# Turning the hidden blocks of the SwiGLU layers on TensorE in place of VectorE blocks and GpSimd transfers

## The chip, the cores and the metric

The kernel runs as one program on one core of a Trainium2 chip. The metric is the device time of one launch in microseconds (us), lower is better. Engines are named as the profile names them: PE is TensorE (PEld its weight loads), DVE is VectorE, ACT is ScalarE, POOL is GpSimd, SP is SyncE, which here only issues transfers. PSUM is the accumulator memory that PE writes; it has 8 banks of 512 float32 per partition (`ps[:, bank, :]` in the code).

## The reference

A two-layer decoder trunk on 256 tokens of width 2048: an RWKV-7 time-mixing layer, then a block-sparse attention layer, and after each mixer a layer norm, a SwiGLU feed-forward network and another layer norm. The change is in the feed-forward part alone:

```python
def _swiglu(x, w_gate, w_up, w_down):
    return (jax.nn.silu(x @ w_gate) * (x @ w_up)) @ w_down

for layer in range(DEPTH):          # DEPTH = 2
    mixed = ...                     # RWKV-7 in layer 0, attention in layer 1
    h = _layernorm(ALPHA * h + mixed, ln1_w[layer], ln1_b[layer])
    h = _layernorm(ALPHA * h + _swiglu(h, ffn_w_gate[layer], ffn_w_up[layer], ffn_w_down[layer]),
                   ln2_w[layer], ln2_b[layer])
```

`x` is 256 x 2048, `w_gate` and `w_up` are 2048 x 5632, `w_down` is 5632 x 2048, all float32.

## The kernel before

**Matmuls.** All projections have one form. A weight matrix is cut into chunks of 256 rows by 512 columns (512 KB, two row tiles of 128). A job is one output block of 512 columns for all 256 tokens: 8 chunks where the inner size is 2048 (`CJ`), 22 where it is 5632 (`CF`). Precision is kept by splitting both operands into a high and a low part of type float32r: each product is three matmuls, high by high, high by low and low by high (`chunk`, L629 to L644, lines L641, L642, L643). The activations are the 128x128 stationary operand, the weights the 512 moving columns, so a chunk is 2 row tiles x 2 token tiles x 3 = 12 matmuls of 512 columns. Odd and even jobs write PSUM banks 0 and 1, or 2 and 3.

**The ring of weights.** SP loads the chunks into a ring of four slots, `raw` (L355, and L397 for `w_down`). ACT copies each to its high part `whi` (`split_hi`, L1310), once it has landed (`raw_landed`) and PE has used the chunk four before it (`chunk_used`). DVE subtracts to get the low part `wlo` (`split_lo`, L1761; in the down projection the same operation in `residual`, L2095) and signals `split_done`, which PE waits for ahead of each chunk and which frees the slot of `raw` for SP.

**The feed-forward part.** For each layer the stage `up` works on the 5632 hidden columns in 11 blocks of 512 (`FB`). A block is two jobs: the gate job into banks 0 and 1, the up job into banks 2 and 3. After the gate job ACT computes Silu of the banks into `gtmp` (token on the partitions, L1636; block 0 has the same operation outside the loop). After the up job DVE multiplies `gtmp` by the other two banks (`multiply`, L2198). The down projection needs the result with the hidden index on the partitions, as stationary operand: `hThi` and `hTlo`. So each block of 256 tokens x 512 hidden columns is turned:

- DVE turns 32x32 squares within each partition group, two instructions for the two token tiles, into `hB` (L2201), and signals `h_blocked`.
- POOL issues 16 transfers from SBUF to SBUF per block, which carry the squares to the right partitions, into `hR` (`turn_hidden`, L605); they signal `h_landed`.
- ACT copies `hR` to the high part `hThi` (`hidden_hi`, L1620), and DVE subtracts for `hTlo` (`hidden_lo`, L2206), which signals `hlo_done`.

Block 0 of a layer is made by `normed_job`, ahead of a loop of 10 (`Fori(0, FB - 1)`) for blocks 1 to 10. ACT and DVE turn block i while PE works on block i + 1: `hidden_hi` stands right behind Silu of the next block in ACT's queue. Block 10 is turned during the down projection: its `hidden_hi` comes after `BEHIND` = 8 further chunks in ACT's queue, and PE needs its result at chunk 20 of 22 of the first down job. The squares leave the hidden index in a permuted order, four hidden rows to a partition; so SP loads `w_down` in the matching order (`blocks`, L392 to L398).

**What sets the order.** Each engine runs its queue in the order written; semaphores tie them together. PSUM banks 4 to 7 are used by the layer norms' turns (`turned`, L1141, PE transposes of 128x128 float32), and by attention, whose PE transposes (L1202) stand between the chunks of the q and output projections. They are idle in the stages `up` and `down`. The whole program has 8 stages in the order proj, wo, up0, down0, kvq, ao, up1, down1.

Of the kernel before, what the change touches and what calls it, by code (L numbers as in the profile page):

```python
# [23 lines left out]
F32 = mybir.dt.float32  # L24
F32R = mybir.dt.float32r
ALU = mybir.AluOpType
# [3 lines left out]
P = 128  # L30
D = 2048
T = 256
# [7 lines left out]
KC = 2  # L40
RING = 4
PLAIN = 2
BEHIND = 8
# [118 lines left out]
def trunk(nc, x, rows, rwkv_rows, lora, w, consts, ln_rows, y):  # L162
    with ExitStack() as ctx:
# [117 lines left out]
        hB = carve(common, 16 * KB, 16, TT, 32)  # L281
        hR = carve(common, 20 * KB, 4, 4, TT, 32)
# [58 lines left out]
        h_blocked, h_landed, hhi_done, hlo_done = (sem(n) for n in ("h_blocked", "h_landed", "hhi_done", "hlo_done"))  # L341
# [8 lines left out]
        def _(sp):  # L350
# [36 lines left out]
            def blocks(c0, mats, kt, n, n0=0):  # L387

                per = len(mats) * kt // KC
                if per % RING:  # L390
                    with sp.Fori(0, n // 2) as i:
                        for b in range(2):  # L392
                            for j in range(kt // KC):
                                c = b * (kt // KC) + j
                                rows = mats[0][j // 2 * 4 * P:(j // 2 + 1) * 4 * P, bass.ds(i * (2 * NB) + (n0 + b) * NB, NB)]
                                sp.wait_ge(split_done, i * (2 * per) + (c0 + c) - (RING - 1))
                                sp.dma_start(raw[:, c % RING], rows.rearrange("(p k) n -> p k n", k=4)[:, j % 2 * KC:(j % 2 + 1) * KC]  # L397
                                             ).then_inc(raw_landed[c % RING], 16)  # L398
                else:
                    with sp.Fori(0, n) as i:  # L400
                        stream(i * per + c0, mats, kt, bass.ds(i * NB + n0 * NB, NB))
# [68 lines left out]
        def _(pool):  # L470
# [129 lines left out]
            def turn_hidden(i):  # L600

                pool.wait_ge(h_blocked, i + 1)
                for a in range(4):
                    for q in range(4):
                        nc.gpsimd.dma_start(hR[32 * q:32 * (q + 1), a], hB[32 * a:32 * (a + 1), 4 * q:4 * (q + 1)]).then_inc(h_landed, 16)  # L605

            for t in range(TT):
                root(0, t)
            for i in range(FB):
                turn_hidden(i)  # L610
# [7 lines left out]
            for i in range(FB, 2 * FB):  # L618
                turn_hidden(i)
# [10 lines left out]
        def _(pe):  # L630
# [539 lines left out]
            def ffn(layer):  # L1170
                c0, j0 = PH[f"up{layer}"]
                u0 = layer * FB

                normed_job(2 * layer, f"up{layer}")
                with pe.Fori(0, FB - 1) as i:
                    job(i * (2 * CJ) + (c0 + 2 * CJ), i + (j0 // 2 + 1), 0, KT, ahi, alo)
                    job(i * (2 * CJ) + (c0 + 3 * CJ), i + (j0 // 2 + 1), 1, KT, ahi, alo)
                c, j = PH[f"down{layer}"]
                pe.wait_ge(hlo_done, u0 + FB - 1)
                pe.wait_ge(bank_free[0], j // 2 + 1)  # L1180
                for ch in range(CF):
                    if ch == CF - KC:
                        pe.wait_ge(hlo_done, u0 + FB)
                    chunk(c, ch, 0, FT, hThi, hTlo)
                job(c + CF, j // 2, 1, FT, hThi, hTlo)
                last_two(c + 2 * CF, j + 2, FT, hThi, hTlo)
# [109 lines left out]
        def _(act):  # L1296
# [317 lines left out]
            def ffn(layer):  # L1614
# [3 lines left out]
                def hidden_hi(i, f0):  # L1618
                    act.wait_ge(h_landed, i * 256 + 256)
                    A(hThi[:, f0, :].rearrange("p f (t a j) -> p f t a j", t=TT, a=4), hR.rearrange("p a f t j -> p f t a j"),  # L1620
                      ACT.Copy).then_inc(hhi_done, 1)
# [7 lines left out]
                with act.Fori(0, FB - 1) as i:  # L1629
# [4 lines left out]
                    act.wait_ge(h_blocked, i + (u0 + 1))  # L1634
# [5 lines left out]
                split_hi(c, c // RING, BEHIND)  # L1640
                hidden_hi(u0 + FB - 1, slice((FB - 1) * 4, FB * 4))
                split_hi(c + BEHIND, c // RING, NJ * CF - RING - BEHIND - layer * 2 * RING)
# [85 lines left out]
        def _(dve):  # L1728
# [349 lines left out]
            def residual(c0, kt, n):  # L2078
# [6 lines left out]
                at = c0 + RING + {0: 9, 1: BEHIND, 2: 2 * CJ - RING, 3: BEHIND}[n]  # L2085
# [104 lines left out]
            def ffn(layer):  # L2190
# [3 lines left out]
                def multiply(c_end, up_seen):  # L2194

                    dve.wait_ge(bank_free[0], up_seen)
                    dve.wait_ge(chunk_used, c_end)
                    V.tensor_tensor(gtmp, gtmp, ps[:, 2:4, :], ALU.mult).then_inc(bank_free[1], 1)  # L2198
                    dve.wait_ge(bank_free[1], up_seen)
                    for t in range(TT):  # L2200
                        last = V.transpose(hB[:, :, t], gtmp[:, t].rearrange("p (q i f) -> p q f i", q=4, f=4))  # L2201
                    last.then_inc(h_blocked, 1)

                def hidden_lo(i, f0):
                    dve.wait_ge(hhi_done, i + 1)
                    V.tensor_tensor(hTlo[:, f0, :].rearrange("p f (t a j) -> p f t a j", t=TT, a=4), hR.rearrange("p a f t j -> p f t a j"),  # L2206
                                    hThi[:, f0, :].bitcast(F32).rearrange("p f (t a j) -> p f t a j", t=TT, a=4),
                                    ALU.subtract).then_inc(hlo_done, 1)
# [9 lines left out]
                split_lo(PH[f"down{layer}"][0] + RING, BEHIND)  # L2218
# [122 lines left out]
```

## Time and profile before

| what | value |
|---|---|
| time, median of 3 runs | 2440.54 us (2440.26 to 2443.91) |
| the profiled execution's own time | 2440.26 us |
| its span, first to last instruction | 2438.5 us |
| PE busy | 2418.4 us, 99% |
| DVE busy | 1443.3 us, 59% |
| ACT busy | 1068.9 us, 44% |
| POOL busy | 309.7 us, 13% |
| mean traffic | 186 GB/s, 452.45 MB |

The span is 1.8 us shorter than the execution's own time, which has what lies before the first and after the last instruction. The matmul durations in the profile are latencies of a pipeline: they overlap, so how fast PE works is read from the starts of its instructions, which follow each other at a smaller distance than one lasts. The stage up0 runs in the trace from 593 us (the transposes of its layer norm) to 1077, down0 from 1077 to 1317, up1 from 1705 to 2188, and down1 from there to the end. Attention's transposes between chunks lie between 1520 and 1640 us.

### The profile page before, as it was taken

How to read it: one execution, taken by the hardware profiler on the slowest of the kernel's cores; microseconds unless marked ns; L12 is line 12 of the kernel's file. 1: busy time of each engine (PE TensorE's matmuls, PEld its weight loads, DVE VectorE, ACT ScalarE, POOL GpSimd, SP SyncE). 2: the span in 40 equal slices, each digit the busy share in tenths (PEclk: the TensorE clock that was granted, in tenths of full speed). 3: DMA queues.
4: the chain of work that ended last, by engine and by line, in shares of the span. 5: the costliest groups of instructions: out<-in, count | busy, mean ns of one | idle time of the engine just before them, and what ended most of it. 6: DMA issues, size and time to landing. Idle time of an engine off the chain costs nothing.

```text
span 2438.5 us, 39415 instructions
## 1 busy us (share of the span) xinstructions
PE 2418.4 (99%) x15364; PEld 1983.1 (81%) x15364; DVE 1443.3 (59%) x1725; ACT 1068.9 (44%) x1345; POOL 309.7 (13%) x536
## 2 busy tenths in 40 slices
PE   9999999999999999999999999999999999999998
PEld 6888778877888888888887888888788888888886
DVE  7788566666755555555446544665855555555445
ACT  4454455444444444444334444553544444444332
POOL 2000235420112121120000000000111212111000
PEclk9999999999999999999999999999999999999999
DMA  7556411266666666666666665455666766667664
GB/s 240 189 192 212 131 42 46 59 211 200 200 204 209 200 204 207 205 208 195 194 192 208 199 195 192 141 177 183 188 202 204 208 204 208 202 203 233 194 195 147
DMA packets 237774, 452.45 MB, mean 186 GB/s; under 512 B 19328, under 2 KB 31040, under 8 KB 236560
## 3 DMA queue, kind: packets, MB, share of 16 engines
q1 hardware_dynamic: 222304, 417.38, 55.3%
q0 software_dynamic: 14944, 33.11, 4.2%
q8 instruction: 91, 1.49, 0.2%
q14 instruction: 35, 0.29, 0.0%
q10 hardware_dynamic: 400, 0.18, 0.0%
HBM read 436.96 MB, written 2.10 MB: 180 GB/s over the span
## 4 chain that ended last, share of the span: by engine, by line
PE 97%; DMA 2%; DVE 1%; issue 0%; ACT 0%; POOL 0%; SPq 0%; DVEq 0%; ACTq 0%
PE ps L643 26%; PE ps L641 26%; PE ps L642 26%; PE ps L965 3%; PE ps L858 1%; PE ps L846 1%; PE ps L1151 1%; PE ps L668 1%; PE ps L670 1%; PE ps L669 1%; PE ps L909 1%; PE ps L811 1%; PE ps L955 1%; DMA raw<-w_k 1%; PE ps L1251 1%; PE ps L992 1%
## 5 line engine op out<-in xcount | busy, mean ns | idle before, releaser
L1310 ACT CAST whi<-raw 128x1024 fp32r<-128x1024 f32 x738 | 775.9, 1052 | 1131.4 <-PE ps L643 1070.5
L1761 DVE TENSOR_TENSOR wlo<-raw,whi 128x1024 fp32r<-128x1024 f32 x569 | 691.9, 1222 | 583.1 <-ACT whi L1310 580.9
L641 PE MATMUL ps<-whi,ahi 128*128 128x512 f32 x2184 | 855.1, 392 | 0.0
L643 PE MATMUL ps<-whi,alo 128*128 128x512 f32 x2184 | 850.7, 390 | 0.0
L642 PE MATMUL ps<-wlo,ahi 128*128 128x512 f32 x2184 | 850.4, 389 | 0.0
L642 PEld LDWEIGHTS ps<-wlo,ahi 128*128 128x128 f32 x2184 | 410.2, 188 | 85.7 <-issue 1.2
L641 PEld LDWEIGHTS ps<-whi,ahi 128*128 128x128 f32 x2184 | 410.2, 188 | 85.5 <-issue 1.2
L643 PEld LDWEIGHTS ps<-whi,alo 128*128 128x128 f32 x2184 | 410.2, 188 | 85.1
L2095 DVE TENSOR_TENSOR wlo<-raw,whi 128x1024 fp32r<-128x1024 f32 x179 | 219.0, 1224 | 227.4 <-ACT whi L1310 226.1
L605 POOL DMA_DIRECT2D common<-common x352 | 172.0, 497 | 818.0 <-DVE common L2201 739.1
L641 PE MATMUL ps<-whi,hThi 128*128 128x512 f32 x656 | 255.4, 389 | 0.0
L642 PE MATMUL ps<-wlo,hThi 128*128 128x512 f32 x656 | 255.4, 389 | 0.0
L643 PE MATMUL ps<-whi,hTlo 128*128 128x512 f32 x656 | 255.4, 389 | 0.0
L643 PEld LDWEIGHTS ps<-whi,hTlo 128*128 128x128 f32 x656 | 123.2, 188 | 25.6
L641 PEld LDWEIGHTS ps<-whi,hThi 128*128 128x128 f32 x656 | 123.2, 188 | 25.5
L642 PEld LDWEIGHTS ps<-wlo,hThi 128*128 128x128 f32 x656 | 123.2, 188 | 25.3
L595 POOL TENSOR_TENSOR rstd<-var,small 128x1 f32<-128x1 f32 x8 | 5.3, 665 | 582.7 <-DVE var L2133 582.7
L965 PE MATMUL ps<-raw,big 128*128 128x256 f32 x256 | 68.8, 400 | 0.1
L965 PEld LDWEIGHTS ps<-raw,big 128*128 128x128 f32 x256 | 44.5, 189 | 7.5 <-ACT big L1456 0.2
L1593 ACT ACTIVATE a2t<-ps,lnT 128x128 f32<-128x128 f32 x96 | 33.8, 549 | 30.7 <-PE ps L1141 30.7
L1926 DVE TENSOR_TENSOR rec<-ps,big 128x512 f32<-128x512 f32 x40 | 27.5, 688 | 32.6 <-PE ps L846 32.6
L2201 DVE STREAM_TRANSPOSE common<-common 128x512 f32<-128x512 f32 x44 | 45.2, 1066 | 0.8
(317 smaller groups left out, 1937.6 us busy)
## 6 DMA issues: line engine op xcount, KB each, us to landing
raw<-w_up SPq DMA_DIRECT2D x176, 512.0 KB, 4.4
raw<-w_down SPq DMA_DIRECT2D x176, 512.0 KB, 4.0
raw<-w_gate SPq DMA_DIRECT2D x172, 512.0 KB, 3.7
raw<-w_k SPq DMA_DIRECT2D x32, 512.0 KB, 4.3
raw<-w_r SPq DMA_DIRECT2D x32, 512.0 KB, 4.3
raw<-w_v SPq DMA_DIRECT2D x32, 512.0 KB, 3.6
raw<-w_o SPq DMA_DIRECT2D x32, 512.0 KB, 4.8
raw<-kv_v SPq DMA_DIRECT2D x32, 512.0 KB, 3.6
```

The costliest lines, as they stand in the source:

```text
L605: nc.gpsimd.dma_start(hR[32 * q:32 * (q + 1), a], hB[32 * a:32 * (a + 1), 4 * q:4 * (q + 1)]).then_inc(h_landed, 16)
L641: mm(o, hi[:, k, tok], whi[:, s, k2, :], start=(k == 0), stop=False)
L642: mm(o, hi[:, k, tok], wlo[:, s, k2, :], start=False, stop=False)
L643: last = mm(o, lo[:, k, tok], whi[:, s, k2, :], start=False, stop=(k == kt - 1))
L668: mm(ps[:, 2 + t, :], hi[:, k, tok], wh[:, k2, :], start=False, stop=False)
L965: last = mm(ps[:, 3, t * T:(t + 1) * T], xxT[:, k, t * P:(t + 1) * P], rawf[:, s, k % FK], start=(i == 0), stop=(k == KT - 1), skip_group_ ...
L1310: nc.scalar.copy(whi[:, s], src).then_inc(hi_done, 1)
L1593: ins = A(hF[:, k, t * P:(t + 1) * P], ps[:, 4 + b, k2 * P:(k2 + 1) * P], ACT.Identity, scale=lnT[:, (n * 2) * KT + k:(n * 2) * KT + k + 1 ...
L1761: V.tensor_tensor(wlo[:, s], src, whi[:, s].bitcast(F32), ALU.subtract).then_inc(split_done, 1)
L1926: V.tensor_tensor(Z.rearrange("p l (j c) -> p l j c", c=CHUNK), ps[:, 0:2, 0:4 * CHUNK].rearrange("p l (j c) -> p l j c", c=CHUNK), mask_l ...
L2095: V.tensor_tensor(wl, raw[:, s], wh.bitcast(F32), ALU.subtract).then_inc(split_done, 1)
L2201: last = V.transpose(hB[:, :, t], gtmp[:, t].rearrange("p (q i f) -> p q f i", q=4, f=4))
```

## The change

The turn of a hidden block moves to PE. A new function `h_transposes(i)` issues 8 transposes of 128x128 (4 hidden tiles x 2 token tiles) from `gtmp` into banks 4 and 5, after a wait for the multiply (`bank_free[1]`), and signals `h_tr`. In the loop it stands between the gate job and the up job; for the last block, between chunks 1 and 2 of the first down job. ACT's `hidden_hi` and DVE's `hidden_lo` now read the banks in place of `hR`. The Silu of the next block waits for `h_tr` where it waited for `h_blocked`, and PE waits at the end of each turn of the loop for `hlo_done`, which says that the banks have been read. DVE's two square turns per block and POOL's 16 transfers per block go, with their buffers. The order of the hidden index is now the plain one, so `w_down` is loaded like every other matrix, and for block 10 `hidden_hi` and `hidden_lo` come after 1 further chunk in place of 8.

```diff
--- before.py
+++ after.py
@@ -40,7 +40,6 @@
-BEHIND = 8
@@ -278,8 +277,6 @@
-        hB = carve(common, 16 * KB, 16, TT, 32)
-        hR = carve(common, 20 * KB, 4, 4, TT, 32)
@@ -338,7 +335,7 @@
-        h_blocked, h_landed, hhi_done, hlo_done = (sem(n) for n in ("h_blocked", "h_landed", "hhi_done", "hlo_done"))
+        h_tr, hhi_done, hlo_done = (sem(n) for n in ("h_tr", "hhi_done", "hlo_done"))
@@ -392,10 +389,8 @@
                         for b in range(2):
                             for j in range(kt // KC):
                                 c = b * (kt // KC) + j
-                                rows = mats[0][j // 2 * 4 * P:(j // 2 + 1) * 4 * P, bass.ds(i * (2 * NB) + (n0 + b) * NB, NB)]
-                                sp.wait_ge(split_done, i * (2 * per) + (c0 + c) - (RING - 1))
-                                sp.dma_start(raw[:, c % RING], rows.rearrange("(p k) n -> p k n", k=4)[:, j % 2 * KC:(j % 2 + 1) * KC]
-                                             ).then_inc(raw_landed[c % RING], 16)
+                                chunk(i * (2 * per) + (c0 + c), c % RING,
+                                      mats[0][j * KC * P:(j + 1) * KC * P, bass.ds(i * (2 * NB) + (n0 + b) * NB, NB)])
                 else:
                     with sp.Fori(0, n) as i:
                         stream(i * per + c0, mats, kt, bass.ds(i * NB + n0 * NB, NB))
@@ -597,17 +592,8 @@
             load_wb(0, z_tr, KT // KC)
             nc.gpsimd.memset(small[:, 0:1], -0.5).then_inc(half_set, 1)
             pool.wait_ge(half_set, 1)
-            def turn_hidden(i):
-
-                pool.wait_ge(h_blocked, i + 1)
-                for a in range(4):
-                    for q in range(4):
-                        nc.gpsimd.dma_start(hR[32 * q:32 * (q + 1), a], hB[32 * a:32 * (a + 1), 4 * q:4 * (q + 1)]).then_inc(h_landed, 16)
-
             for t in range(TT):
                 root(0, t)
-            for i in range(FB):
-                turn_hidden(i)
             root(1, 0)
             load_wb(1, chunk_used, PH["kvq"][0])
             root(1, 1)
@@ -615,8 +601,6 @@
             load_wb(2, qk_tr, STEPS)
             for t in range(TT):
                 root(2, t)
-            for i in range(FB, 2 * FB):
-                turn_hidden(i)
             pool.wait_ge(chunk_used, PH["down1"][0])
             nc.gpsimd.dma_start(wb_last, lnw(3)).then_inc(wb_in, 16)
             for t in range(TT):
@@ -1171,10 +1155,20 @@
                 c0, j0 = PH[f"up{layer}"]
                 u0 = layer * FB
 
+                def h_transposes(i):
+
+                    pe.wait_ge(bank_free[1], i + (j0 // 2 + 2 - u0))
+                    for f in range(4):
+                        for t in range(TT):
+                            last = tr(ps[:, 4 + f // 2, (f % 2) * T + t * P:(f % 2) * T + (t + 1) * P], gtmp[:, t, f * P:(f + 1) * P], ident[:])
+                    last.then_inc(h_tr, 1)
+
                 normed_job(2 * layer, f"up{layer}")
                 with pe.Fori(0, FB - 1) as i:
                     job(i * (2 * CJ) + (c0 + 2 * CJ), i + (j0 // 2 + 1), 0, KT, ahi, alo)
+                    h_transposes(i + u0)
                     job(i * (2 * CJ) + (c0 + 3 * CJ), i + (j0 // 2 + 1), 1, KT, ahi, alo)
+                    pe.wait_ge(hlo_done, i + (u0 + 1))
                 c, j = PH[f"down{layer}"]
                 pe.wait_ge(hlo_done, u0 + FB - 1)
                 pe.wait_ge(bank_free[0], j // 2 + 1)
@@ -1182,6 +1176,8 @@
                     if ch == CF - KC:
                         pe.wait_ge(hlo_done, u0 + FB)
                     chunk(c, ch, 0, FT, hThi, hTlo)
+                    if ch == 1:
+                        h_transposes(u0 + FB - 1)
                 job(c + CF, j // 2, 1, FT, hThi, hTlo)
                 last_two(c + 2 * CF, j + 2, FT, hThi, hTlo)
 
@@ -1616,9 +1612,8 @@
                 u0 = layer * FB
 
                 def hidden_hi(i, f0):
-                    act.wait_ge(h_landed, i * 256 + 256)
-                    A(hThi[:, f0, :].rearrange("p f (t a j) -> p f t a j", t=TT, a=4), hR.rearrange("p a f t j -> p f t a j"),
-                      ACT.Copy).then_inc(hhi_done, 1)
+                    act.wait_ge(h_tr, i + 1)
+                    A(hThi[:, f0, :], ps[:, 4:6, :].rearrange("p a (k t) -> p (a k) t", k=2), ACT.Copy).then_inc(hhi_done, 1)
 
                 split_hi(c0 + RING, c0 // RING + 1, CJ)
                 act.wait_ge(chunk_used, c0 + CJ)
@@ -1631,15 +1626,15 @@
                     u = i * (2 * CJ // RING) + (c0 + 2 * CJ) // RING
                     split_hi(c + RING, u + 1, CJ)
 
-                    act.wait_ge(h_blocked, i + (u0 + 1))
+                    act.wait_ge(h_tr, i + (u0 + 1))
                     act.wait_ge(chunk_used, c + CJ)
                     A(gtmp, ps[:, 0:2, :], ACT.Silu).then_inc(bank_free[0], 1)
                     hidden_hi(i + u0, bass.ds(i * 4, 4))
                     split_hi(c + (RING + CJ), u + (1 + CJ // RING), CJ)
                 c = PH[f"down{layer}"][0] + RING
-                split_hi(c, c // RING, BEHIND)
+                split_hi(c, c // RING, 1)
                 hidden_hi(u0 + FB - 1, slice((FB - 1) * 4, FB * 4))
-                split_hi(c + BEHIND, c // RING, NJ * CF - RING - BEHIND - layer * 2 * RING)
+                split_hi(c + 1, c // RING, NJ * CF - RING - 1 - layer * 2 * RING)
 
             norm_affine(0, PH["up0"][0])
             ffn(0)
@@ -2082,7 +2077,7 @@
-                at = c0 + RING + {0: 9, 1: BEHIND, 2: 2 * CJ - RING, 3: BEHIND}[n]
+                at = c0 + RING + {0: 9, 1: 1, 2: 2 * CJ - RING, 3: 1}[n]
@@ -2196,16 +2191,11 @@
                     dve.wait_ge(bank_free[0], up_seen)
                     dve.wait_ge(chunk_used, c_end)
                     V.tensor_tensor(gtmp, gtmp, ps[:, 2:4, :], ALU.mult).then_inc(bank_free[1], 1)
-                    dve.wait_ge(bank_free[1], up_seen)
-                    for t in range(TT):
-                        last = V.transpose(hB[:, :, t], gtmp[:, t].rearrange("p (q i f) -> p q f i", q=4, f=4))
-                    last.then_inc(h_blocked, 1)
 
                 def hidden_lo(i, f0):
                     dve.wait_ge(hhi_done, i + 1)
-                    V.tensor_tensor(hTlo[:, f0, :].rearrange("p f (t a j) -> p f t a j", t=TT, a=4), hR.rearrange("p a f t j -> p f t a j"),
-                                    hThi[:, f0, :].bitcast(F32).rearrange("p f (t a j) -> p f t a j", t=TT, a=4),
-                                    ALU.subtract).then_inc(hlo_done, 1)
+                    V.tensor_tensor(hTlo[:, f0, :], ps[:, 4:6, :].rearrange("p a (k t) -> p (a k) t", k=2),
+                                    hThi[:, f0, :].bitcast(F32), ALU.subtract).then_inc(hlo_done, 1)
 
                 natural_and_split(2 * layer, c0)
                 with dve.Fori(0, FB - 1) as i:
@@ -2215,7 +2205,7 @@
                     hidden_lo(i + u0, bass.ds(i * 4, 4))
                     split_lo(c + (RING + CJ), CJ)
                 multiply(c0 + FB * 2 * CJ, j0 // 2 + FB + 1)
-                split_lo(PH[f"down{layer}"][0] + RING, BEHIND)
+                split_lo(PH[f"down{layer}"][0] + RING, 1)
                 hidden_lo(u0 + FB - 1, slice((FB - 1) * 4, FB * 4))
 
             residual(PH["wo"][0], KT, 0)
```

On PE, at the end of the gate job in the loop of the stage up0. The kernel before (L641 to L643 are the matmuls of `chunk`, L636 the wait of the next job):

```order
L641 MATMUL ps<-whi,ahi 128x512
L642 MATMUL ps<-wlo,ahi 128x512
L643 MATMUL ps<-whi,alo 128x512
L636 REGISTER_ALU [waits bank_free1]
L641 MATMUL ps<-whi,ahi 128x512 [waits split_done]
```

The changed kernel, at the same place (L625 to L627 are the matmuls of `chunk`, `common` is the memory in which `gtmp` lies):

```order
L625 MATMUL ps<-whi,ahi 128x512
L626 MATMUL ps<-wlo,ahi 128x512
L627 MATMUL ps<-whi,alo 128x512
L1163 MATMUL ps<-ident,common 128x128 [waits bank_free1]
L1163 MATMUL ps<-ident,common 128x128 x7
L620 REGISTER_ALU [waits bank_free1]
L625 MATMUL ps<-whi,ahi 128x512 [waits split_done]
```

Eight instructions, the first with a wait, stand between the two jobs; nothing else on PE has moved.

On ACT, after the loop, at the start of the down projection of layer 0. The kernel before (L1310 is the copy of a chunk's high part, L1620 is `hidden_hi` of block 10):

```order
L1310 CAST whi<-raw 128x1024 [waits chunk_used,raw_landed2]
L1310 CAST whi<-raw 128x1024 [waits chunk_used,raw_landed3]
L1620 ACTIVATE hThi<-common 128x1024 [waits h_landed]
L1310 CAST whi<-raw 128x1024 [waits chunk_used,raw_landed0]
L1310 CAST whi<-raw 128x1024 [waits chunk_used,raw_landed1]
```

The changed kernel, from the end of the loop (L1624) on (L1306 is the copy, L1616 is `hidden_hi`):

```order
L1624 REGISTER_ALU
L1624 COMPARE_AND_BRANCH
L1306 CAST whi<-raw 128x1024 [waits chunk_used,raw_landed0]
L1616 ACTIVATE hThi<-ps 128x1024 [waits h_tr]
L1306 CAST whi<-raw 128x1024 [waits chunk_used,raw_landed1]
```

`hidden_hi` of block 10 is now the second operation after the loop, behind one copy; before, eight copies stood ahead of it.

## Rows read from the trace of the kernel before

**Rows 1.** The page: busy time, granted clock by slice of the span.

```profile
PE 2418.4 (99%) x15364; PEld 1983.1 (81%) x15364; DVE 1443.3 (59%) x1725; ACT 1068.9 (44%) x1345; POOL 309.7 (13%) x536
...
PEclk9999999999999999999999999999999999999999
```

**Rows 2.** Stretches: busy us and instructions (x) by engine, clock, DMA share, GB/s.

```profile
560.00:640.00 80.00, 80.00 (x356) 63.93 (x355) 58.44 (x67) 37.80 (x58) 1.12 (x2) 1.00 0.60 186
640.00:1080.00 440.00, 440.00 (x1943) 364.54 (x1942) 239.91 (x203) 187.84 (x182) 78.25 (x160) 1.00 0.69 205
1345.00:1510.00 165.00, 165.00 (x730) 136.70 (x729) 81.16 (x65) 72.14 (x71) 0.00 (x0) 1.00 0.61 195
1510.00:1640.00 130.00, 129.99 (x657) 109.55 (x656) 80.85 (x106) 65.16 (x122) 0.53 (x1) 1.00 0.49 163
```

**Rows 3.** Waits from 640 to 1080 us: in total, times, longest.

```profile
ACT whi L1310 <- PE ps L643: 252.2, 152, 1.7
DVE wlo L1761 <- ACT whi L1310: 192.9, 132, 1.5
```

**Rows 4.** Timeline of PE, first transposes of attention: start, us, what.

```profile
1518.04 0.39 PE L643 MATMUL ps<-whi,alo 128*128 128x512 f32 x1
...
1520.08 0.39 PE L643 MATMUL ps<-whi,alo 128*128 128x512 f32 x1
1520.31 1.03 PE L1202 MATMUL ps<-ident,big 128*128 128x128 f32 x8
1521.10 0.48 PE L641 MATMUL ps<-whi,ahi 128*128 128x512 f32 x1
1521.41 0.40 PE L642 MATMUL ps<-wlo,ahi 128*128 128x512 f32 x1
...
1523.69 0.39 PE L643 MATMUL ps<-whi,alo 128*128 128x512 f32 x1
```

**Rows 5.** Timeline of PE, the next group of eight transposes.

```profile
1533.21 0.40 PE L643 MATMUL ps<-whi,alo 128*128 128x512 f32 x1
1533.44 1.04 PE L1202 MATMUL ps<-ident,big 128*128 128x128 f32 x8
...
1536.86 0.39 PE L643 MATMUL ps<-whi,alo 128*128 128x512 f32 x1
```

**Rows 6.** Line L1202, PE: duration ns min/median/max.

```profile
L1202 PE MATMUL ps<-ident,big x64: 270/273/276, 1520.3 to 1625.6; 128*128 128x128 f32 x64
```

**Rows 7.** Timeline of ACT, then of DVE: end of a gate job in up0.

```profile
661.20 1.05 ACT L1310 CAST whi<-raw 128x1024 fp32r<-128x1024 f32 x1 [1.67 <-PE ps L643]
663.92 1.05 ACT L1310 CAST whi<-raw 128x1024 fp32r<-128x1024 f32 x1 [1.67 <-PE ps L643]
664.87 1.02 ACT L1636 ACTIVATE common<-ps 128x1024 f32<-128x1024 f32 x1
665.79 1.05 ACT L1620 ACTIVATE hThi<-common 128x1024 f32 x1
666.74 1.04 ACT L1310 CAST whi<-raw 128x1024 fp32r<-128x1024 f32 x1
...
662.28 1.23 DVE L1761 TENSOR_TENSOR wlo<-raw,whi 128x1024 fp32r<-128x1024 f32 x1 [1.50 <-ACT whi L1310]
667.01 1.23 DVE L2206 TENSOR_TENSOR hTlo<-common,hThi 128x1024 f32 x1 [0.78 <-ACT hThi L1620]
```

**Rows 8.** Timeline of PE, DVE and ACT, start of down0.

```profile
1077.16 0.39 PE L641 MATMUL ps<-whi,hThi 128*128 128x512 f32 x1
...
1079.59 1.21 DVE L2198 TENSOR_TENSOR common<-common,ps 128x1024 f32<-128x1024 f32 x1
...
1082.85 1.05 ACT L1310 CAST whi<-raw 128x1024 fp32r<-128x1024 f32 x1 [1.67 <-PE ps L643]
```

**Rows 9.** The page: what the change takes out.

```profile
L605 POOL DMA_DIRECT2D common<-common x352 | 172.0, 497 | 818.0 <-DVE common L2201 739.1
L2201 DVE STREAM_TRANSPOSE common<-common 128x512 f32<-128x512 f32 x44 | 45.2, 1066 | 0.8
```

**Rows 10.** DMA issues: KB each, median us from issue to landing.

```profile
raw<-w_up SPq DMA_DIRECT2D x176, 512.0 KB, 4.4
raw<-w_down SPq DMA_DIRECT2D x176, 512.0 KB, 4.0
```

**Rows 11.** Timeline of PE, first layer norm's transposes, and what follows them.

```profile
603.46 0.79 PE L641 MATMUL ps<-whi,ahi 128*128 128x512 f32 x1
604.09 0.40 PE L642 MATMUL ps<-wlo,ahi 128*128 128x512 f32 x1
```

## Prediction, made before the changed kernel ran

> **What bounds the kernel now.** I read the page first, then a table of stretches, the waits inside one stretch, and the timeline of PE. The page shows PE busy for 99% of the span and its granted clock at the upper level, 2.4 GHz, in every slice [rows 1]. Durations of matmuls overlap, so the busy share alone could hide a slow stream. The starts do not: nine steps from 1518.04 to 1520.08 us make 2.04 us, 0.227 us for a matmul of 512 columns [rows 4]. The stretches say the same of the stage that is changed: 440 us hold 1943 matmuls, 0.226 us each, and the stretch from 1345 to 1510, in which POOL does nothing and no square is turned, holds 730 in 165 us, 0.226 us each [rows 2]. So beside DVE's turns and POOL's transfers PE runs as fast as without them. A chunk of 12 matmuls is 2.72 us.
>
> Who waits for whom between 640 and 1080 us: ACT waits 252.2 us for PE, in 152 pieces of up to 1.7 us, and DVE 192.9 us for ACT; no wait of PE is in the list [rows 3]. The ring is full and PE empties it. How far ahead it is: a copy starts at 661.20 us, DVE's subtraction behind it ends at 663.51 [rows 7], 2.3 us after the copy's start. The copy starts when PE has used one chunk, and PE needs the new one three chunks later, 8.2 us. The margin is about 5.8 us.
>
> **The change, part by part.**
>
> What goes: 44 square turns on DVE, 45.2 us, and 352 small transfers on POOL, 172.0 us of issuing [rows 9]. Neither engine sets the end, DVE is busy for 59% and POOL for 13% of the span [rows 1], and PE waits for neither in this stage. Worth on the path: nothing. If PE did wait for them unseen, it would show as a step above that of the stretch without them, and the step is the same [rows 2]. So the bounds of this term are 0 and 0.
>
> What comes: per block 8 transposes of 128x128 float32 on PE, which is the path itself. Nothing hides them. There are 10 blocks in the loop and one behind it, in two layers: 22 groups, 176 transposes. Attention has the same groups in the same surroundings: eight transposes of float32 against the identity into banks 4 and 5, between two float32r chunks. The price of a group can be read in three ways:
> - From the first transpose at 1520.31 to the second matmul after them at 1521.41 is 1.10 us, of which 0.227 is the step of a matmul: 0.87 us [rows 4].
> - From the last matmul before to the twelfth after them, 1520.08 to 1523.69, is 3.61 us; twelve steps are 2.72: 0.89 us [rows 4]. It has in it the few slightly longer steps that follow.
> - The same at the second group, 1533.21 to 1536.86: 3.65 less 2.72, 0.93 us [rows 5].
>
> I take 0.89, because the first group stands between plain jobs as the new ones will, while DVE and ACT do softmax work around the second. 22 x 0.89 = 19.6 us. The ends are 22 x 0.87 = 19.1 and 22 x 0.93 = 20.5 us.
>
> The waits that the change adds on PE:
> - `bank_free[1]` ahead of the transposes in the loop: the multiply is done right after the block's own up job, a whole gate job (21.8 us) before. Behind it on PE stands everything, but it is met.
> - The same ahead of the last group, in the down projection: PE starts down0 at 1077.16 and would reach the group after two chunks, at 1082.60; the multiply runs from 1079.59 to 1080.80 [rows 8]. Margin 1.8 us.
> - `hlo_done` at the loop's end: `hidden_lo` ends at 668.24 [rows 7]; the loop's end is a whole up job (21.8 us) behind the end of the gate job at 663.7, near 685.5. Margin 17 us.
>
> The waits on ACT: Silu now needs `h_tr`, 0.87 us after the end of the gate job. A copy starts at that end, at 663.92, so `h_tr` comes near 664.79; Silu starts behind that copy at 664.87 anyway [rows 7]. Behind it `hidden_hi` and the next copy keep their places, and that copy's chunk on PE is itself 0.87 us later. Cost 0.
>
> The reads of PSUM in place of SBUF: `hidden_hi` reads 1024 elements per partition from SBUF in 1.05 us, and Silu as many from PSUM in 1.02; `hidden_lo` takes 1.23 from SBUF, the multiply with one operand in PSUM 1.21 [rows 7, 8]. No difference, and off the path.
>
> `hidden_hi` of block 10, earlier in the queue: `h_tr` comes near 1082.60 + 0.87 = 1083.5, so the copy of chunk 5, which stood at 1082.85 [rows 8], starts near 1084.6 behind `hidden_hi`. DVE has `hidden_lo` between, and finishes the chunk near 1087.2. PE wants it at 1077.16 + 5 x 2.72 + 0.87 = 1091.6. Margin 4.4 us. The refill of that slot starts 2 us later than now, takes 4.0 us to land [rows 10], and its next copy has to wait for PE until about 1094.3. Cost 0. If these covers were gone, each microsecond of lateness would cost one, twice in the program.
>
> `w_down` in plain row order: the same 176 transfers of 512 KB, on the same queue; they land in 4.0 us now and those of `w_up`, which have the plain order, in 4.4 [rows 10]. The 0.4 us are inside the margin of the ring. Cost 0.
>
> Sum against the profiled execution: 2440.26 + 19.6 = 2459.9 us. The median of the three runs is 0.3 us above that execution, so 2460 us for the median.
>
> **The rivals.**
>
> 1. *A transpose costs its whole duration.* The row of the line gives 273 ns for one [rows 6]. If each stood alone on the engine, 176 x 0.273 = 48.0 us: 2488.3 us. Against it: the eight of a group stand in 0.79 us from the first start to the next matmul's [rows 4], 0.10 us each, so they overlap. It would take a reason for which those in the loop don't. I give it 3 in 100.
> The Trainium skill, in "TensorE: Matmul & The Clock Gate", Part 4: PE-mode transpose, gives about 275 ns for a transpose in a kernel's context, and says that transposes do not count as activity for the clock as matmuls do. By that rule the time would be that of this rival, with a fall of the clock possibly on top. The trace agrees with the duration and not with the cost, since the starts are 0.10 us apart; and the clock reads 1.00 both in the stretch of attention and in the one with 16 transposes in a row twice [rows 2].
>
> 2. *The change of kind is dearer in the loop.* After the layer norm's float32 work the first float32r matmul takes a step of 0.63 us (603.46 to 604.09) [rows 11], 0.40 more than usual, the dearest change of kind near this stage. In the loop the transposes also stand behind a wait against a register, which attention's don't have, and a second such wait closes the loop. If each group paid 0.40 more, 22 x 0.40 = 8.8: 2468.7 us. Against it: that step follows matmuls of 512 float32 columns, and eight transposes are followed by one of 0.31 [rows 4]; and each chunk begins with a wait in the same way now, with no mark on the step. 4 in 100.
>
> 3. *Not slower: PE's step is set by the supply of chunks.* If the ring delivered a chunk every 2.72 us, the transposes would fill time in which PE now waits, and the chunks would come when they come. It decides once a chunk becomes ready less than 0.87 us before its use. The time would then be 2440.3 us, or a little less, as POOL's transfers no longer share the DMA engines. For it: the DMA share is 0.69 in the stage, against 0.61 without the squares [rows 2]. Against it: the margin of 5.8 us, ACT waiting for PE and not for landings [rows 3], and the equal step in both stretches [rows 2]. 2 in 100.
>
> **How the numbers follow.** My forecast has 91 in 100: 2460 us, with 2459.4 to 2460.8 by the ends of the price, and a few tenths to a microsecond or two for things that I count as nothing. Rival 2 has 4, rival 1 has 3, rival 3 has 2. The range is 2457.5 to 2466: it takes in half of what rival 2 costs and leaves the rest out. A change of 0.2% is 4.9 us, about what a measurement of this kernel can tell from none. The forecast and rivals 1 and 2 lie above it, together 98; rival 3 is split between no change and faster, 1 each.
>
> **What would show each step.** In the profile of the changed kernel 176 transposes more on PE in 22 groups of 8, in the two stages up and at the start of each down projection. The start-to-start distance over a group and the twelve matmuls behind it should be 3.61 us. PE should have no idle time ahead of a group, the granted clock should stay at 1.00, the step elsewhere at 0.227 us, and each turn of the loop should be 0.89 us longer than 43.5. POOL should be idle in the stages, and DVE's busy time about 45 us lower. I am wrong if the groups cost much over 0.93 us, if the matmul step in other places changes, or if the span grows by another amount than the groups add up to.

## The result and the profile after

The changed kernel takes 2460.46 us (median of 6 runs, 2459.0 to 2461.51); the kernel before took 2440.4 us in its 6 (2437.9 to 2443.91). The ratio is 1.0081, with a 95% interval of 1.007 to 1.009. It is 20.1 us slower, and 2460 us were forecast.

The page of the changed kernel, busy time and what its transfers and DVE's turns left [rows 1, 9, 10]:

```profile
PE 2438.2 (99%) x15540; PEld 2000.3 (81%) x15540; DVE 1404.0 (57%) x1681; ACT 1071.2 (44%) x1345; POOL 137.6 (6%) x184
...
PEclk9999999999999999999999999999999999999999
...
raw<-w_up SPq DMA_DIRECT2D x176, 512.0 KB, 3.6
raw<-w_down SPq DMA_DIRECT2D x176, 512.0 KB, 4.1
```

PE has 176 instructions more and 19.8 us more busy time. DVE is 39.3 us lower, not 45 as forecast: the lengths of its instructions add up to 46.5 us less, but they overlap in part, less so here than before (46.1 us in all against 53.3). POOL is 172.1 us lower. The clock is the same.

The stretch of stage up0 and the one without transposes, of the changed kernel [rows 2], then the waits in the stage [rows 3]:

```profile
640.00:1080.00 440.00, 440.00 (x1983) 365.08 (x1982) 217.64 (x179) 185.30 (x179) 0.00 (x0) 1.00 0.65 189
...
1349.00:1514.00 165.00, 165.00 (x729) 136.64 (x728) 84.83 (x68) 72.86 (x71) 0.00 (x0) 1.00 0.61 195
```

```profile
ACT whi L1306 <- PE ps L627: 255.5, 159, 1.7
DVE wlo L1756 <- ACT whi L1306: 215.1, 159, 1.5
```

No wait of PE is in this list either. DVE now waits 22 us longer for ACT, about its 20.5 us of square turns in this stretch: it does nothing with the time that it got.

The timeline of PE at the first group of the loop, and at the second [rows 4, 5]:

```profile
664.90 0.39 PE L627 MATMUL ps<-whi,alo 128*128 128x512 f32 x1
665.13 1.03 PE L1163 MATMUL ps<-ident,common 128*128 128x128 f32 x8
665.92 0.48 PE L625 MATMUL ps<-whi,ahi 128*128 128x512 f32 x1
666.24 0.40 PE L626 MATMUL ps<-wlo,ahi 128*128 128x512 f32 x1
...
709.32 0.40 PE L627 MATMUL ps<-whi,alo 128*128 128x512 f32 x1
709.55 1.04 PE L1163 MATMUL ps<-ident,common 128*128 128x128 f32 x8
...
712.96 0.39 PE L627 MATMUL ps<-whi,alo 128*128 128x512 f32 x1
```

Nothing is idle ahead of the eight. From 709.32 to 712.96 are 3.64 us, which with the unrounded starts is 3.65: 0.93 us over twelve steps of 0.2267. The first group costs 0.89. From the first group to the second are 44.42 us (665.13 to 709.55) and from there to the third 44.44, against 43.52 for a turn of this loop in the kernel before: 0.9 more, as forecast. Over all 22 groups, measured in this way, the sum is 20.0 us: 12 groups of 0.89 and 10 of 0.93.

The profiled execution took 2461.66 us, 21.4 more than that of before. When the starts of PE's common instructions are laid side by side, the offset is 1.4 us from 600 us on, behind the first layer norm and ahead of anything that is changed; it grows by 0.89 or 0.93 at each of the 22 groups and elsewhere moves by less than 0.1 us. So 1.4 us is how two executions differ in their first stages, and 20.0 us is the change.

### The profile page after: what moved, and what is told of

Same layout as the page of the kernel before. It is cut to its first block, busy times and chain, and to the rows that moved or that the text cites. A ratio compares the mean times of both kernels' runs of the same rounds, so it can differ in the third digit from the quotient of the medians.

```text
span 2459.9 us, 39371 instructions
## 1 busy us (share of the span) xinstructions
PE 2438.2 (99%) x15540; PEld 2000.3 (81%) x15540; DVE 1404.0 (57%) x1681; ACT 1071.2 (44%) x1345; POOL 137.6 (6%) x184
## 4 chain that ended last, share of the span: by engine, by line
PE 98%; DMA 1%; DVE 1%; issue 0%; ACT 0%; DVEq 0%; SPq 0%; ACTq 0%
PE ps L627 26%; PE ps L625 26%; PE ps L626 26%; PE ps L949 3%; PE ps L842 1%; PE ps L830 1%; PE ps L1135 1%; PE ps L1163 1%; PE ps L654 1%; PE ps L653 1%; PE ps L652 1%; PE ps L893 1%; PE ps L795 1%; PE ps L939 1%; DMA big<-x 1%; PE ps L976 1%
## 5 line engine op out<-in xcount | busy, mean ns | idle before, releaser
L1306 ACT CAST whi<-raw 128x1024 fp32r<-128x1024 f32 x738 | 776.3, 1052 | 1141.4 <-PE ps L627 1088.0
L625 PE MATMUL ps<-whi,ahi 128*128 128x512 f32 x2184 | 856.3, 392 | 0.0
L627 PE MATMUL ps<-whi,alo 128*128 128x512 f32 x2184 | 850.3, 389 | 0.0
L627 PEld LDWEIGHTS ps<-whi,alo 128*128 128x128 f32 x2184 | 409.9, 188 | 85.5
L625 PEld LDWEIGHTS ps<-whi,ahi 128*128 128x128 f32 x2184 | 410.0, 188 | 85.2 <-issue 1.2
L625 PE MATMUL ps<-whi,hThi 128*128 128x512 f32 x656 | 255.4, 389 | 0.0
L627 PE MATMUL ps<-whi,hTlo 128*128 128x512 f32 x656 | 255.2, 389 | 0.0
L627 PEld LDWEIGHTS ps<-whi,hTlo 128*128 128x128 f32 x656 | 123.1, 188 | 25.7
L625 PEld LDWEIGHTS ps<-whi,hThi 128*128 128x128 f32 x656 | 123.1, 188 | 25.5
L1765 DVE SCALAR_TENSOR_TENSOR big<-big,mixT 128x256 f32<-128x256 f32 x96 | 40.7, 480 | 0.5
L2197 DVE TENSOR_TENSOR hTlo<-ps,hThi 128x1024 f32 (+1 forms) x22 | 26.9, 1224 | 19.5 <-ACT hThi L1616 19.5
```

The lines of the kernel that those rows point to most:

```text
L625: mm(o, hi[:, k, tok], whi[:, s, k2, :], start=(k == 0), stop=False)
L627: last = mm(o, lo[:, k, tok], whi[:, s, k2, :], start=False, stop=(k == kt - 1))
L1306: nc.scalar.copy(whi[:, s], src).then_inc(hi_done, 1)
L1765: return V.scalar_tensor_tensor(out=out, in0=xxT[:, k], scalar=mixT[:, m * KT + k:m * KT + k + 1], in1=xT[:, k, 1:T + 1], op0=ALU.mult, op ...
L2197: V.tensor_tensor(hTlo[:, f0, :], ps[:, 4:6, :].rearrange("p a (k t) -> p (a k) t", k=2), hThi[:, f0, :].bitcast(F32), ALU.subtract).then_ ...
```

## The experiments

Each kernel is given as what it changes in the changed kernel, or in the kernel before where it says so. The four of the first round share runs of the kernel before (median 2440.39 us), the three of the second share others (2441.0 us).

**One transpose per group.** In `h_transposes` the loops keep the last of the eight:

```diff
-                    for f in range(4):
-                        for t in range(TT):
+                    for f in range(3, 4):
+                        for t in range(1, TT):
```

> The changed kernel with 1 of the 8 transposes in each of the 22 groups; the other seven are left out, so most of the turned block is stale. All waits, PSUM reads and the rest of the change stay. Theory (a transpose costs its step on PE, 0.109 us, and the change of kind next to nothing): a group costs 0.109 + 0.02 to 0.05, 22 groups 2.9 to 3.5 us, so 2443.5 us, 17 us below the changed kernel. Rival (a group has a fixed price, for the change from float32r to float32 and back or for its waits, of about half of the 0.89 us): 22 x 0.5 = 11 us, so 2451 us.

Measured: 2443.62 us, ratio 1.0012 (1.0003 to 1.0022). The timeline of PE at a group of this kernel:

```profile
667.63 0.39 PE L627 MATMUL ps<-whi,alo 128*128 128x512 f32 x1
667.87 0.27 PE L1163 MATMUL ps<-ident,common 128*128 128x128 f32 x1
667.89 0.47 PE L625 MATMUL ps<-whi,ahi 128*128 128x512 f32 x1
668.21 0.39 PE L626 MATMUL ps<-wlo,ahi 128*128 128x512 f32 x1
```

A place with one transpose costs 0.14 or 0.16 us, in turn. All new waits, the PSUM reads of ACT and DVE and the other row order of `w_down` are in this kernel, and 3.2 us are all that it adds (0.7 to 5.4 by the interval); the 22 places add up to 3.3 us in the trace. The fixed price of half is refuted.

The profiled execution is the slowest of the ten, 2447.73 us, 7.5 over that of before. Of these 4.1 us lie ahead of 640 us, where this kernel does the same as the one before. With the starts laid side by side, 1.8 us of that are lost from 318 to 327 us, around a stretch in which the granted clock was at the lower level for most of the time:

```profile
322.00:326.00 4.00, 4.00 (x98) 3.23 (x98) 1.39 (x4) 0.00 (x0) 3.92 (x6) 0.57 0.00 0
```

PE had paused for 1.34 us just before, among the short matmuls of the RWKV layer. In the trace of the changed kernel a pause of 1.33 us at 396.6 us, in the same layer, left the clock at 1.00.

**Sixteen transposes per group.**

```diff
-                    for f in range(4):
+                    for f in range(8):
+                        f = f % 4
                         for t in range(TT):
```

> The changed kernel with each group's 8 transposes issued twice, 16 in a row into the same places. Theory: 8 more at 0.109 us, 22 times: 19.2 us more than the changed kernel, 2479.7 us. Rival (fixed price of about half): the second eight cost about 0.45 us a group, 10 us more, 2470 us. Rival (PE has hidden slack of its supply, so that the first eight were partly free): the second eight cost more than the first, over 20.5 us more.

Measured: 2479.61 us, ratio 1.0162 (1.0145 to 1.0179). The second eight cost 19.2 us, 0.109 us each, so the first eight were neither partly free nor mostly a fixed price. The timeline shows the sixteen in 1.66 us, from their first start to the next matmul's:

```profile
663.18 1.91 PE L1164 MATMUL ps<-ident,common 128*128 128x128 f32 x16
664.84 0.48 PE L625 MATMUL ps<-whi,ahi 128*128 128x512 f32 x1
```

**The turn left out of the kernel before.**

```diff
-                for a in range(4):
-                    for q in range(4):
+                for a in range(3, 4):
+                    for q in range(3, 4):
                         nc.gpsimd.dma_start(hR...
...
-                    act.wait_ge(h_landed, i * 256 + 256)
+                    act.wait_ge(h_landed, i * 16 + 16)
...
-                    for t in range(TT):
+                    for t in range(1, TT):
                         last = V.transpose(hB...
```

> The kernel before with the turn's work almost all left out: DVE turns one of the two token tiles, POOL issues 1 of the 16 transfers per block, and ACT waits for that one; the block that ACT and DVE split is stale for the most part. Nothing is added to PE. Theory (what the change takes off DVE, POOL and the DMA engines is worth nothing on the path): the time of the kernel before, 2440.4 us within 1.5. Rival (the removed work did slow PE or the ring, and the transposes cost more than the 20 us of the difference): below it by 3 us or more, 2437 us or less.

Measured: 2440.16 us, ratio 1.0 (0.9991 to 1.001). The starts of PE's matmuls keep their distance from those of the kernel before within 0.05 us from 640 us to the end. In the same stretch as [rows 2], POOL has 5.04 us in place of 78.25, and the number of matmuls is the same 1943:

```profile
640.00:1080.00 440.00, 440.00 (x1943) 364.46 (x1942) 231.21 (x193) 187.81 (x182) 5.04 (x10) 1.00 0.67 194
```

Half of DVE's turns and one transfer in sixteen are still in this kernel; what was left out of it, and it is most of what the change takes off, was free.

**The group ahead of the gate job.**

```diff
+                    h_transposes(i + u0)
                     job(i * (2 * CJ) + (c0 + 2 * CJ), i + (j0 // 2 + 1), 0, KT, ahi, alo)
-                    h_transposes(i + u0)
```

> The changed kernel with the group of the loop moved ahead of the gate job, right behind the up job whose result it needs; nothing is left out. Now the wait for the multiply bites: in the trace of before PE starts the gate job at 641.96 us and the multiply ends at 645.65, 3.7 us later. Theory (PE sets the end, so every idle microsecond on it counts, whatever the ring holds ready): 20 blocks x 3.7 to 3.9 us, 74 to 78 us more than the changed kernel, about 2536 us. Rival (the step of PE is the supply's, with PE able to catch up): the 3.7 us are inside the ring's margin of 5.8 us and vanish, about 2461 us. In between if PE's work behind the wait is faster for a while.

Measured: 2573.7 us, ratio 1.0546 (1.0529 to 1.0564). That is 113.2 us over the changed kernel, not 74 to 78. The rival is refuted, and the theory is short by 37 us. The timeline of PE at the first group shows why:

```profile
643.44 0.39 PE L627 MATMUL ps<-whi,alo 128*128 128x512 f32 x1
647.41 1.97 PE L1163 MATMUL ps<-ident,common 128*128 128x128 f32 x8 [3.58 <-DVE common L2193]
649.03 0.78 PE L625 MATMUL ps<-whi,ahi 128*128 128x512 f32 x1
649.60 0.63 PE L626 MATMUL ps<-wlo,ahi 128*128 128x512 f32 x1
650.03 0.63 PE L627 MATMUL ps<-whi,alo 128*128 128x512 f32 x1
```

and the stretch around it, with the granted clock ahead of the DMA share:

```profile
644.00:653.00 9.00, 5.59 (x17) 4.74 (x18) 2.36 (x2) 0.96 (x1) 0.00 (x0) 0.63 0.43 125
```

PE waits 3.7 us for the multiply, as worked out. Behind the wait the transposes take 0.20 us each and the matmuls step by 0.43, about twice as long: the granted clock has a mean of 0.63 here, that is, it fell to its lower level of 1.2 GHz for part of the stretch. Then it comes back. Per block 113.2 / 20 = 5.7 us: 3.7 of idle time and 2.0 of work at the lower clock.

The 2.0 us are a mean. The clock fell at each of the 20 waits, during the wait or up to 1.2 us behind its end, and came back sooner at some than at others. A wait with its group costs 7.4 to 7.5 us at 7 of the 20, this one among them, and 5.9 to 6.3 at the other 13. With 3.7 of idle time and 0.91 for the group alone it would be 4.6. At the fourth group the eight transposes still run at the upper level, 0.11 us each, and the matmuls behind them at the lower:

```profile
798.88 1.10 PE L1163 MATMUL ps<-ident,common 128*128 128x128 f32 x8 [3.53 <-DVE common L2193]
...
800.48 0.63 PE L627 MATMUL ps<-whi,alo 128*128 128x512 f32 x1
800.91 0.63 PE L625 MATMUL ps<-whi,ahi 128*128 128x512 f32 x1
```

**The group behind the first chunk.** The job is written out, with the group behind its chunk 0:

```diff
-                    job(i * (2 * CJ) + (c0 + 2 * CJ), i + (j0 // 2 + 1), 0, KT, ahi, alo)
-                    h_transposes(i + u0)
+                    pe.wait_ge(bank_free[0], i + (j0 // 2 + 2))
+                    for ch in range(CJ):
+                        chunk(i * (2 * CJ) + (c0 + 2 * CJ), ch, 0, KT, ahi, alo)
+                        if ch == 0:
+                            h_transposes(i + u0)
```

> The changed kernel with the loop's group behind the first chunk of the gate job. The multiply ends 3.7 us after the job's start and a chunk is 2.7 us, so PE should idle for 1.0 us in each of 20 blocks. Theory (the 37.5 us by which the group ahead of the gate job cost more than its idle time are those of a granted clock that falls after an idle time of 3.7 us): after 1.0 us of idling the clock stays at the upper level, and only the idle time is added: 20 x 1.0 = 20 us over the changed kernel, 2480 us, with the matmuls behind the group at 0.227 us. Rival (any wait ahead of a group brings the slow matmuls): 20 x (1.0 + 1.9) = 58 us more, 2518 us, with matmuls at 0.427 us behind the group.

Measured: 2480.94 us, ratio 1.0166 (1.015 to 1.0181), 20.5 us over the changed kernel. The timeline of PE at the first group:

```profile
643.09 0.39 PE L627 MATMUL ps<-whi,alo 128*128 128x512 f32 x1
644.35 1.09 PE L1163 MATMUL ps<-ident,common 128*128 128x128 f32 x8 [0.87 <-DVE common L2196]
645.19 0.48 PE L625 MATMUL ps<-whi,ahi 128*128 128x512 f32 x1
645.51 0.39 PE L626 MATMUL ps<-wlo,ahi 128*128 128x512 f32 x1
```

PE starts the group 1.03 us late (0.98 at 18 of the 20), and what follows has the usual steps. So an idle microsecond costs one. The clock stayed at the upper level behind all 20 of these waits and fell at all 20 of the longer ones.

**Single transposes between chunks.** The job is written out again. One transpose stands behind each of chunks 2 to 7 and two more behind the last; `h_some` is `h_transposes` cut into parts, with the wait at the first and the signal at the last:

```diff
+                    for ch in range(CJ):
+                        chunk(i * (2 * CJ) + (c0 + 2 * CJ), ch, 0, KT, ahi, alo)
+                        if ch >= 2:
+                            h_some(i + u0, ch - 2, ch - 1)
+                    h_some(i + u0, 6, 8)
```

> The changed kernel with the loop's eight transposes spread over the second half of the gate job: one behind each of chunks 2 to 7 and two more at the end; the group in the down projection stays. Nothing is left out. Theory (a place costs 0.04 us for its change of kind beside 0.109 a transpose, as 1 transpose cost 0.14 to 0.16 us and 8 cost 0.89 to 0.93): six more places per block, 20 x 6 x 0.04 = 5 us over the changed kernel, 2465 us. Rival (a change of kind is free and the 0.04 us are noise of the steps): 2460.5 us, no difference. Rival (each place costs 0.314 - 0.227 = 0.09 us, as its first step looks): 20 x 6 x 0.09 = 10.5 us, 2471 us.

Measured: 2463.33 us, ratio 1.0092 (1.0077 to 1.0107), 2.9 us over the changed kernel (2.3 if each is taken against its own runs of the kernel before). The expectation counted the places wrongly: the last single and the two behind it are one place of three, so there are 5 places more per block, not 6. In the trace a single costs 0.152 us on average (0.14 or 0.16) and a three 0.347; per block 5 x 0.152 + 0.347 = 1.107 us against 0.910, and 20 x 0.197 = 3.9 us. Of the three accounts only the theory's fits, with 0.04 us for a place: 20 x 5 x 0.04 = 4 us. A difference of 3 us between kernels of different rounds is near what these runs can tell, so the verdict rests on the trace more than on the times.

**K of attention turned off PE**, in the kernel before. The changes, without the places of the buffers:

```diff
-                    for n in range(4):
-                        last = tr(ps[:, 4 + h, n * P:(n + 1) * P], (Qn, Kn)[n // 2][:, n % 2, hs], ident[:])
+                    for n in range(TT):
+                        last = tr(ps[:, 4 + h, n * P:(n + 1) * P], Qn[:, n, hs], ident[:])
...
+                    k = kR[i // 2][:, :, (2 * i + h) % 4]
+                    mm(ps[:, 6 + h, 0:P], qkt[:, h, 0:P], k[:, :, 0], start=True, stop=True)
+                    last = mm(ps[:, 6 + h, P:3 * P], qkt[:, h, P:2 * P], k.rearrange("p a t j -> p t a j"), start=True, stop=True)
...
+            for b in range(NJ):
+                for t in range(TT):
+                    split_lo(q0 + RING + b * TT + t, 1, (b * TT + t) % RING)
+                    last = V.transpose(kB[b][:, :, t], Kn[:, t, b * NB:(b + 1) * NB].rearrange("p (h q i) -> p q h i", h=4, q=4))
+                last.then_inc(k_blocked, 1)
```

POOL gets a loop of 4 x 16 transfers from `kB` to `kR`, as `turn_hidden` has, and `scores` a wait for them.

> The kernel before, with its own trade carried further: of attention's 64 PE transposes the 32 of K go. DVE turns K in 32x32 squares between the chunks of the first q job (8 instructions), POOL carries them over in 64 transfers into memory that is idle then, and the score matmuls read K from there, as a moving operand in runs of 32 elements. Nothing is left out. Theory (a float32 transpose costs 0.109 us on PE, and DVE's and POOL's work beside it nothing): 32 x 0.109 = 3.5 us less than the kernel before, 2436.9 us. Rival (the runs of 32 elements slow the score matmuls): they are 16 of 128 and 16 of 256 columns, 0.11 and 0.22 us each, 5.2 us in all; at half the pace they take 5.2 us more, 2442 us. Rival (the squares on DVE push the ring late in the q job): PE idles there, and a microsecond or more comes back.

Measured: 2437.35 us (median of 11 runs) against 2441.0, ratio 0.9986 (0.9977 to 0.9996). This is the fastest of the kernels here, by 3.6 us over the kernel before (1.0 to 5.6 by the interval). When the starts of PE's other matmuls in the two traces are laid side by side, 3.4 us are gained between 1515 and 1640 us, about 0.44 at each step of attention, against 3.5 forecast. The lines of it for the transposes and scores, and DVE's turns:

```profile
L1210 PE MATMUL ps<-ident,big x32: 270/272/275, 1519.6 to 1621.4; 128*128 128x128 f32 x32
...
L1223 PE MATMUL ps<-common,big x32: 379/380/382, 1525.7 to 1628.8; 128*128 128x256 f32 x32
...
L2281 DVE STREAM_TRANSPOSE big<-big x6: 703/704/706, 1505.7 to 1519.3; 128x512 f32<-128x512 f32 x6
```

PE has half of the 64 transposes of [rows 6]. The score matmuls of 256 columns last 380 ns, as they do in the kernel before (381). Since that is a latency, the starts have to be read too. From the first score matmul of a step to the next matmul of the projection, in this kernel:

```profile
1525.50 0.38 PE L1222 MATMUL ps<-common,big 128*128 128x128 f32 x2
...
1526.62 0.58 PE L649 MATMUL ps<-whi,ahi 128*128 128x512 f32 x1
```

and in the kernel before:

```profile
1526.64 0.38 PE L1212 MATMUL ps<-big 128*128 128x128 f32 x2
...
1527.76 0.58 PE L641 MATMUL ps<-whi,ahi 128*128 128x512 f32 x1
```

Both are 1.12 us, so the runs of 32 elements cost nothing. The expectation was off in what the scores take in all: each of these float32 matmuls stands twice in the trace, so 8 steps are 9 us and not 5.2, and the rival at half the pace would have been that much dearer. The other rival is out as well: PE is busy for all of the 20 us from 1500 to 1520, while DVE turns the squares.

## Why the prediction was right, step by step

- *What bounds the kernel.* PE, without slack. Shown by the group ahead of the gate job and the one behind the first chunk: idle time on PE is added to the end in full, whatever the ring holds ready. Rival 3 (the supply sets the step) is refuted by both.
- *What goes is worth nothing.* Shown by leaving most of it out of the kernel before: ratio 1.0. The loads of `w_up` land in 3.6 us now against 4.4 [rows 10], which looks like the work of POOL's transfers. But with one transfer in sixteen left they still took 4.2 us, so what slowed them is not shown. Either way the ring's margin hid it.
- *22 groups at 0.89 us.* The term of the sum. The trace has 0.89 at 12 and 0.93 at 10 of them, 20.0 us together, against 19.6 forecast with ends of 19.1 and 20.5. The reason I gave for taking 0.89 alone, that softmax work had made attention's second group dearer, was wrong: the two values also take turns in the loop, in which no softmax runs. By 1, 8 and 16 transposes the price is 0.109 us for each and 0.02 to 0.05 for a place. That the forecast of 2460 us lies within 0.5 us of the median is in part luck, since single executions of the changed kernel are spread over 2.5 us.
- *Rival 1, a transpose at its whole 273 ns,* would have been 48 us. The transposes have the same duration, and the sixteen in 1.66 us show that they overlap; the clock stayed at the upper level with sixteen in a row too.

```profile
L1163 PE MATMUL ps<-ident,common x176: 270/272/273, 665.1 to 2215.2; 128*128 128x128 f32 x176
```

- *Rival 2, a dearer change of kind.* Refuted: the first step behind a group is 0.32 us in the loop (665.92 to 666.24), as in attention, and the one-transpose kernel bounds all that is not transposes. (The prediction says that its range takes in half of what this rival costs. It takes in more: 2466 is 6.1 us above the sum, of 8.8.)
- *The added waits.* None bites. The last group of layer 0 follows its multiply with the margin that was worked out. The timelines of DVE and PE in the changed kernel at the start of down0 [rows 8]:

```profile
1090.10 1.21 DVE L2193 TENSOR_TENSOR common<-common,ps 128x1024 f32<-128x1024 f32 x1
...
1093.11 1.03 PE L1163 MATMUL ps<-ident,common 128*128 128x128 f32 x8
```

The multiply ends at 1091.31, 1.8 us ahead, as forecast. Chunk 5, which now comes behind `hidden_lo` on DVE, is ready at 1097.61 us, and PE gets to it at 1102.16: 4.5 us ahead, against 4.4 forecast. In the loop Silu and `hidden_hi` start right behind the copy, as before [rows 7]:

```profile
665.33 1.05 ACT L1306 CAST whi<-raw 128x1024 fp32r<-128x1024 f32 x1 [1.67 <-PE ps L627]
666.28 1.02 ACT L1631 ACTIVATE common<-ps 128x1024 f32<-128x1024 f32 x1
667.21 1.02 ACT L1616 ACTIVATE hThi<-ps 128x1024 f32 x1
```

- *The price of a lost cover* was given as one microsecond for each of lateness. That holds for a wait of 1.0 us. At 3.7 us the true price was 1.5 times the wait on average, since the clock fell. The statement did not enter the sum, as no cover was lost.

## What to carry to other kernels

Where one engine sets the end and its instructions follow each other without a gap, price a move by what that engine issues more, step by step from the starts of its instructions in a like place, and count what the idle engines are spared as nothing until a run without it says otherwise. A detour by two idle engines and 16 transfers per block can be the faster way, however clumsy it looks; here carrying it into one more stage gained 3.4 us in the trace. When work has to be put on the bound engine, its place matters more than its length: eight transposes cost 0.9 us where their data were ready and 6.6 us on average, with the wait, where they were not.

## What the runs showed of the hardware that was not expected

- PE's granted clock fell to its lower level at each of 20 waits of 3.7 us, and work ran about half as fast for a few microseconds, 1.3 to 2.9 us lost per block beside the wait. Behind 20 waits of 1.0 us between dense matmuls it never fell. Among the short matmuls of the RWKV layer it fell once, behind a pause of 1.34 us, and stayed at 1.00 in another trace behind one of 1.33. What decides between the two is not shown.
- The price of a group alternates between 0.893 and 0.927 us from turn to turn of the loop, that of a single transpose between 0.14 and 0.16. Which of the two comes shows in the next steps (0.227 us each, or up to 0.236 for about ten matmuls). What sets it stays open.
- DVE's square turn of 128x512 elements took 1066 ns on average in the kernel before [rows 9], where it read with a stride of 4 elements, and 704 ns on K, which it reads in runs of 32 neighbours. That the stride is the cause was not tried by itself.
